# Eleven pairs of experts first, fourteen triples last: a new order of units in a mixture of experts

## What is computed

```python
def _moe(x, p):
    scores = jax.nn.sigmoid(xf @ p['w_router'])
    ...   # group-limited choice of 8 of 64 experts for each token
    def expert_block(args):
        h = silu(einsum('td,edf->tef', xb, w_gate)) * einsum('td,edf->tef', xb, w_up)
        h = h * gb[..., None]
        return einsum('tef,efd->td', h, w_down)
    shared = (silu(xf @ ws_gate) * (xf @ ws_up)) @ ws_down
    return routed + shared
```

## Time and profile before

| | before |
|---|---|
| median of three runs | 1019.37 us |
| lowest and highest | 1017.78, 1020.24 us |
| the profiled execution's own time | 1016.32 us |
| its span, first to last instruction | 1014.5 us |
| TensorE busy (modelled) | 915.6 us, 90% |
| bytes moved | 265.11 MB |
| mean granted TensorE clock | 0.964 |

### The profile page before, as it was taken

One profiled execution on the slowest core, in us unless ns is written; L12 is line 12 of the kernel. 1 busy time (PEld: TensorE's weight loads), 2 busy tenths in 40 slices (PEclk: granted clock), 3 DMA queues, 4 the chain that ended last, 5 costly groups with the idle time before them and its releaser, 6 DMA issues.

```text
span 1014.5 us, 19304 instructions
## 1 busy us (share of the span) xinstructions
PE 915.6 (90%) x7879; PEld 552.0 (54%) x7879; DVE 495.6 (49%) x1030; ACT 230.0 (23%) x478; POOL 243.7 (24%) x280
## 2 busy tenths in 40 slices
PE   4999999999999997779999999978889978798995
PEld 4878877887787777536744434323333333233332
DVE  2148857885787487885624333313322323222325
ACT  3231134113411351244111212111211112111213
POOL 0039904960794099100100000000000000000000
PEclk9999999999999999979999999979989989898999
DMA  8643134214412408139688999999999999999961
GB/s 242 188 125 94 36 122 144 62 44 138 126 55 84 139 2 291 27 145 420 273 340 343 394 419 420 419 420 420 418 419 420 419 420 420 420 419 421 420 281 44
DMA packets 76598, 265.11 MB, mean 261 GB/s; under 512 B 12799, under 2 KB 44097, under 8 KB 51656
## 3 DMA queue, kind: packets, MB, share of 16 engines
q1 hardware_dynamic: 72791, 254.16, 64.7%
q0 software_dynamic: 3712, 9.64, 2.5%
HBM read 263.29 MB, written 5.89 MB: 265 GB/s over the span
## 4 chain that ended last, share of the span: by engine, by line
PE 60%; DMA 19%; SPq 9%; DVE 7%; ACT 2%; issue 2%; DVEq 0%; POOLq 0%; ACTq 0%
PE bank L1368 58%; DMA big<-in_w_up 17%; SPq L403 8%; ACT big L1665 2%; DMA big<-in_w_in 1%; PE bank L637 1%; DVE big L1955 1%; DVE big L2008 1%; DVE big L2012 1%; ACT L1665 1%; DMA big<-xg,big 0%; DVE big L920 0%; DVE big L1203 0%; PE bank L700 0%; SPq L467 0%
## 5 line engine op out<-in xcount | busy, mean ns | idle before, releaser
L1368 PE MATMUL bank<-big 64*64 64x64 f32 (+8 forms) x7422 | 858.5, 377 | 78.2 <-DMA big<-in_w_up 42.5
L1368 PEld LDWEIGHTS bank<-big 64*64 64x64 f32 (+5 forms) x7422 | 498.0, 142 | 421.0 <-issue 348.0
L1665 ACT ACTIVATE big<-bank 128x512 f32<-128x512 f32 (+8 forms) x277 | 118.9, 458 | 622.5 <-PE bank L1368 471.0
L1209 POOL DMA_INDIRECT big<-xg,big x25 | 25.0, 998 | 508.2 <-PE bank L637 402.8
L2154 POOL TENSOR_SCALAR big<-big 128x256 f32<-128x256 f32 x120 | 128.2, 1069 | 0.4
L1072 DVE TENSOR_TENSOR big<-big,bank 128x256 f32<-128x256 f32 x25 | 10.6, 422 | 216.1 <-ACT big L1665 216.1
L2166 POOL TENSOR_TENSOR big<-big 128x256 f32<-128x256 f32 x120 | 87.6, 730 | 0.3
L1955 DVE SCALAR_TENSOR_TENSOR big<-big 128x256 f32<-128x256 f32 x120 | 74.7, 623 | 4.1
L1120 DVE TENSOR_TENSOR big<-big,bank 128x512 f32<-128x512 f32 x100 | 68.7, 688 | 12.6 <-PE bank L1368 11.1
L1013 DVE TENSOR_SCALAR big<-bank 128x1 uint32<-128x1 f32 x25 | 4.0, 159 | 114.1 <-PE bank L1368 114.1
L1665 ACT ACTIVATE big<-big 128x272 f32<-128x272 f32 (+9 forms) x109 | 49.9, 502 | 41.5 <-DVE big L1890 11.3
(11 more groups left out here) (156 smaller groups left out, 360.1 us busy)
## 6 DMA issues: line engine op xcount, KB each, us to landing
big<-in_w_gate SPq DMA_DIRECT2D x64, 1024.0 KB, 22.9
big<-in_w_up SPq DMA_DIRECT2D x64, 1024.0 KB, 27.2
big<-in_w_down SPq DMA_DIRECT2D x64, 1024.0 KB, 27.9
big<-in_w_in SPq DMA_DIRECT2D x29, 1024.0 KB, 5.4
big<-in_w_out SPq DMA_DIRECT2D x2, 2048.0 KB, 12.0
big<-in_state_wkv SPq DMA_DIRECT2D x32, 64.0 KB, 2.2
out_wkv_s<-big SPq DMA_DIRECT2D x32, 64.0 KB, 3.9
big<-in_x_prompt SPq DMA_DIRECT2D x2, 512.0 KB, 3.5
```

What stands on the lines that cost most here:

```text
L1209: pool.indirect_dma_start(out=x[0:n, :], out_offset=None, in_=xg, in_offset=bass.IndirectOffsetOnAxis(ap=idxu[0:n, col:col + 1], axis=0), ...
L1368: return nc.tensor.matmul(out_, lhsT=lhsT, rhs=rhs, start=start, stop=stop)
L1665: return nc.scalar.activation(out_, in_, f, **kw)
```

## The change

`UNITS` becomes eleven pairs and then fourteen triples. `FIRST_T` (11) is the first triple. In triples the order on TensorE is index, **combine(q-1)**, gate_up(q), one piece of the shared down product in each of the first five triples (units 11 to 15), turn_gates(q), turn(q+1), turn_hidden(q), down(q). Pairs keep the order they had. ScalarE turns the next unit's tokens ahead of `hidden_turned` in triples, and VectorE adds the last unit's products ahead of `hidden`. The down weights now go through five slots (n % 5), since the sixth keeps the shared expert's until unit 15; gate and up keep six.

```diff
-UNITS = 'PPP' + 'TTP' * 6 + 'TP' * 2
+UNITS = 'P' * 11 + 'T' * 14
...
-        SHARED_SLOT = 5
+        SHARED_SLOT, NDSLOT = 5, 5
...
         def filled_down(n):
-            return n // NSLOT + 1
+            return n // NDSLOT + 1
...
+        FIRST_T = UNITS.index('T')
...
                 if after:
                     sp.wait_ge(S['h_mm'], u + 1)
-                for n in after:
-                    load_item(sp, 0, n % NSLOT, expert_w(0, which[n + NSLOT]))
-                    load_item(sp, 1, n % NSLOT, expert_w(1, which[n + NSLOT]))
+                for m in after:
+                    load_item(sp, 0, m % NSLOT, expert_w(0, which[m]))
+                    load_item(sp, 1, m % NSLOT, expert_w(1, which[m]))
...
-                if after:
+                if after_down:
                     sp.wait_ge(S['yx_mm'], u + 1)
-                for n in after:
-                    load_item(sp, 2, n % NSLOT, expert_w(2, which.pop(n + NSLOT)))
-                if u == 1:
-                    sp.wait_ge(S['shd_mm'], NDOWN)
-                    load_item(sp, 2, SHARED_SLOT, expert_w(2, SHARED_SLOT))
+                for m in after_down:
+                    load_item(sp, 2, m % NDSLOT, expert_w(2, which.pop(m)))
...
+                if q >= FIRST_T:
+                    combine(q - 1)
+                    gate_up(q)
+                    if q < FIRST_T + NDOWN:
+                        shared_down(q - FIRST_T)
+                    turn_gates(q)
+                    if q + 1 < NU_E:
+                        turn(q + 1)
+                    turn_hidden(q)
+                    down(q)
+                    continue
                 gate_up(q)
...
+                if FIRST_T <= q < LAST:
+                    turned(q + 1)
                 hidden_turned(q)
-                if 1 <= q < LAST:
+                if 1 <= q < FIRST_T:
                     turned(q + 1)
...
+                if q >= FIRST_T:
+                    add_late(q - 1)
                 hidden(q)
...
+                if FIRST_T <= q < FIRST_T + NDOWN:
+                    shared_rows(q - FIRST_T)
                 take_gates(q)
```

More of the change, by code:

```diff
@@ L463, in moe_sp @@
             for u in range(NU_E):
-                after = [n for n in members(u) if n + NSLOT < NE]
-                for n in after:
-                    m = n + NSLOT
-                    which[m] = m if m < NSTATIC else sp.value_load(ids[0:1, m:m + 1], min_val=0, max_val=NE - 1)
+                after = [n + NSLOT for n in members(u) if n + NSLOT < NE]
+                after_down = [n + NDSLOT for n in members(u) if n + NDSLOT < NE]
+                for m in after:
+                    which[m] = sp.value_load(ids[0:1, m:m + 1], min_val=0, max_val=NE - 1)
                 if after:
                     sp.wait_ge(S['h_mm'], u + 1)
-                for n in after:
-                    load_item(sp, 0, n % NSLOT, expert_w(0, which[n + NSLOT]))
-                    load_item(sp, 1, n % NSLOT, expert_w(1, which[n + NSLOT]))
+                for m in after:
+                    load_item(sp, 0, m % NSLOT, expert_w(0, which[m]))
+                    load_item(sp, 1, m % NSLOT, expert_w(1, which[m]))
                 if u == 0:
                     sp.wait_ge(S['shg_mm'], 4)
+                    which[SHARED_SLOT] = SHARED_SLOT
                     for part in range(2):
                         load_item(sp, part, SHARED_SLOT, expert_w(part, SHARED_SLOT))
-                if after:
+                if after_down:
                     sp.wait_ge(S['yx_mm'], u + 1)
-                for n in after:
-                    load_item(sp, 2, n % NSLOT, expert_w(2, which.pop(n + NSLOT)))
-                if u == 1:
-                    sp.wait_ge(S['shd_mm'], NDOWN)
-                    load_item(sp, 2, SHARED_SLOT, expert_w(2, SHARED_SLOT))
+                for m in after_down:
+                    load_item(sp, 2, m % NDSLOT, expert_w(2, which.pop(m)))
             sp.wait_ge(S['cnt_ready'], 1)
@@ L566, in shared_down @@
                 wait(pe, 'shy_ready', n if n < 4 else 0)
-                wait(pe, 'cb_sum', 3 if n == 3 else 0)
+                wait(pe, 'cb_sum', NC * (FIRST_T + n))
                 t, h = divmod(n, 2)
@@ L661, in turn_hidden @@
                     pe.wait_ge(S['shh_ready'], 2)
-                if q == 2:
+                if q == FIRST_T + NDOWN - 1:
                     pe.wait_ge(S['shs_ready'], 6)
@@ L672, in down @@
                 for n in members(q):
-                    pe.wait_ge(S[f'wd_in{n % NSLOT}'], 16 * filled_down(n))
+                    pe.wait_ge(S[f'wd_in{n % NDSLOT}'], 16 * filled_down(n))
                 for h in range(2):
@@ L677, in down @@
                             ins = mm(ps_y[h][lo:lo + w, :], hT[:, j, lo:lo + w],
-                                     slot_w[n % NSLOT][1][:, j, 512 * h:512 * h + 512], j == 0, j == 1)
+                                     slot_w[n % NDSLOT][1][:, j, 512 * h:512 * h + 512], j == 0, j == 1)
                 note(ins, 'yx_mm')
@@ L716, in combine @@
                     else:
-                        if n == 2 and q < 2:
-                            pe.wait_ge(S['shy_ready'], (3, 4)[q])
+                        if n == 2 and 0 <= q - FIRST_T < 4:
+                            pe.wait_ge(S['shy_ready'], q - FIRST_T + 1)
                         ins = mm(comb_bank(q, n), GT[q % NGT][:, 128 * t:128 * t + r],
@@ L732, in moe_pe @@
                     turn(1)
-                    shared_down(0)
                     turn_gates(0)
@@ L736, in moe_pe @@
                     down(0)
-                    shared_down(1)
                     continue
-                if q == 1:
-                    shared_down(2)
                 combine(q - 1)
@@ L743, in moe_pe @@
                 turn_gates(q)
-                if q + 1 < NU_E:
-                    turn(q + 1)
+                turn(q + 1)
                 down(q)
-                if q == 1:
-                    shared_down(3)
-                    shared_down(4)
             with pe.If(count > SLOTS):
@@ L850, in moe_act @@
             for q in range(NU_E):
[L851 to L854, removed]
                 if q == 4:
@@ L862, in moe_act @@
                     turned(1)
+                if q == FIRST_T + NDOWN - 1:
+                    act.wait_ge(S['shd_mm'], NDOWN)
+                    for i in range(4):
+                        note(fn(shs[0:NS, QD * i:QD * i + QD], ps_ss[32 * i:32 * i + NS, :], ACT.Copy), 'shs_ready')
+                if FIRST_T <= q < LAST:
+                    turned(q + 1)
                 hidden_turned(q)
-                if 1 <= q < LAST:
+                if 1 <= q < FIRST_T:
                     turned(q + 1)
@@ L1089, in pair @@
                     v.memset(xq, 0.0)
[L1090 to L1095, removed]
+                if 0 < q < FIRST_T:
+                    add_late(q - 1)
+                if FIRST_T <= q < FIRST_T + NDOWN:
+                    shared_rows(q - FIRST_T)
                 take_gates(q)
```

## The result

The changed kernel takes **1030.95 us** (median of four runs, 1029.14 to 1034.18) against 1019.81 us before (four runs): a ratio of 1.0114 with a 95% interval of 1.009 to 1.0138. Run once more beside the experiments it gave 1.0102 (1.0082 to 1.0122). It is slower, as forecast, and the forecast of 1029 was 2 us low. The profiled execution took 1029.14 us with a span of 1027.3.

What follows compares the result with a forecast made beforehand. TensorE bounds the pairs, idling DMA engines; transfers bound the triples. Data from 705.2 plus 106 matrices (280.4 us) gives 985.6; the work behind makes span 1024.3, 9.8 over the old, so 1019.37 + 9.8 = 1029.2; range 1022 to 1038.

Steps and rivals of the forecast that it cites:

- The two numbers that decide: Whole kernel: how long the DMA engines stand idle, and how much work follows the last weights waited for.
- the prediction's other road: Check assuming never-idle DMA engines from 511.3: 174 matrices at 2.645 us land at 971.5, the kernel ends at 1010.2.
- the prediction's never-idle end: End of kernel had the DMA engines never idled from 511.3 us on: 1010.2 us.
- the prediction's bound: Whole kernel: saved TensorE waits cannot bring the end below 1010.2 us, so are worth 4.3 us at most.
- S(0): Start of down in unit 0: predicted at 516.4 us, 518.33 less the 1.93 us shared block.
- S(10): Start of down in unit 10, the last pair: predicted at 687.7 us, ten pairs of 17.13 us after 516.4.
- the row of 17.13: TensorE's time for a unit in its full part, read from the old profile: 17.13 us, pairs and triples alike.
- Rival 1: Whole stream: transfers run nearer their byte rate, 106 matrices land 5.3 us earlier, giving 1022 to 1026 us; 20%.
- Rival 2: Pairs' stage: DMA engines do not idle there, so the end comes 4.3 us down, at 1015 us; 4%.
- Rival 3: Triples: at a mean clock of 0.75 they become bound by TensorE, giving 1036 to 1046 us; 12%.
- 1.7 us of half clock: Tail: products after the last wait for weights run at half clock, adding 1.7 us.
- the price of the sums ahead at the first triple: Unit 11: combine(10) ahead of gate_up(11) releases SyncE later, so the DMA engines idle 4.6 us more.

Runs made afterwards that it cites:

- The cut in pairs: Changed kernel with the four wide combine products of units 0 to 9 cut from 512 to 64 columns, the rest left out: 1016.92 us.
- the same cut in triples: Changed kernel with the combine products of units 12 to 21 cut from 512 to 64 columns instead: 1030.99 us.
- the sorted kernel with the old ends: Changed kernel with the old order in the first triple, unit 11, and the last two units, 23 and 24: 1024.81 us.
- the two settings: Changed kernel with old order in the first triple: 1026.45 us; old units, late pieces, five slots, new order in triples 3, 4, 6, 7 alone: 1015.12 us.
- the best kernel: Kernel before with only the shared pieces moved to the first five triples and five down slots, old units and order: 1010.10 us.

## Why the prediction was right, point by point

**The two numbers that decide.** Right. The cut in pairs (13.0 us) against the same cut in triples (nothing) shows that idle DMA time in the pairs' stage makes the loss. Ahead of the first data of unit 11 the prediction has 14.0 us of it (705.2 - 511.3, less 68 matrices at 2.645); by the trace it is 15.2 (707.64 - 511.99, less 68 at 2.653). With the cut in pairs the last weights waited for were there 462.1 us behind the first data (975.17 - 511.91 - 1.2), and 174 matrices at 2.653 need 461.6: the engines did not idle, as on the prediction's other road.

Sorting the units costs 14.7 us on otherwise like code, near the 14.1 between the forecast and the prediction's never-idle end, and that is in part luck. In the sorted kernel with the old ends the last wait was over at 988.71, with a first issue at 515.01: 472.5 us behind the first data, so 10.9 us were idling and the rest was not split. And the kernel with the old units and the shared pieces late, whose DMA share is 1.00 from 530 to 580 us, has a span of 1009.0, near the never-idle end of 1010.2, but in another way: its last wait is over at 905.06 with 104 us of TensorE's work behind, not at 971.5 with 38.7. Its way from the first issue to the end is 7.4 us shorter than before (497.2 against 504.6), so the prediction's bound, that the saved waits are worth 4.3 us at most, does not hold for every kernel with these parts.

**The terms** (first of the prediction, then of the profile after):

| term | predicted | measured |
|---|---|---|
| shared piece out of unit 0, from the first transfer to S(0) | 1.9 us less | 8.39 to 6.63, 1.8 less |
| S(0) | 516.4 | 518.6, of it 2.05 ahead of the expert stage |
| one pair | 17.13 | 17.25 |
| DMA share in the pairs' stage | near 0.92 | 0.96 (but 390 of 420 GB/s, which is 0.93) |
| from S(10) to the gate of expert 28 | 16.3 | 16.5 |
| that issue | 704.0 | 707.64 |
| idle gap just ahead of the data | 5 to 6 | 5 (703 to 708) |
| TensorE's time of a triple with a shared piece | 20.5 | 20.58 (732.34 - 711.76) |
| each of 106 matrices, landing | 2.645 | (990.02 - 708.84) / 106 = 2.653 |
| last wait for weights over | 985.6 | 990.0 |
| first triple with a wait on in_w_down | about 15, then 4 to 5 us each | 13 (753.5), then 1.9 to 7.4 us each |
| from the last wait for weights to the end | 38.7 | 37.2 |
| span | 1024.3 | 1027.3 |

The 3.0 us between the spans are 2.05 of chance ahead of the stage, 1.2 in ten pairs, 0.8 in 106 matrices and some tenths, less 1.6 in the tail. A pair followed by a pair takes 0.12 us more than a pair followed by a triple, which is what the row of 17.13 was.

**Rival 1** (transfers at their byte rate) is out: 2.653 us again. **Rival 2** (faster, the pairs never idle) is out: 0.96. **Rival 3** (triples become TensorE's through the clock) is out: TensorE waits for weights in every triple from unit 13 to 23. The cut in triples, at a mean grant of 0.88, moves nothing. The Trainium skill, "TensorE: Matmul & The Clock Gate", section "A second HAM failure mode: psum-queue depth-cycling", says of another kernel that frequent short idles between groups of products made the clock swing. The first two triples have such idles (0.49 and 0.78 us a unit) and no long ones, and the stretch from 691 to 753 us was granted 1.00 throughout, TensorE busy 58.07 of 62 us. In these rows idles of that size left the clock at its upper level; the 0.92 further on goes with waits of 1.9 to 7.4 us.

**The tail** was sized with 1.7 us of half clock. In this execution the products behind the last wait of 1.89 us took 3.64 us, at full clock; in the second profile of the same kernel, behind a wait of 1.57, they took 5.32, and its tail was 38.8 us (1028.7 - 989.90), as predicted. So the term comes in some executions of one kernel and not in others; what decides it no run shows.

**Where I was wrong** is what the parts are worth. The schedule takes all five shared pieces out of the pairs' stage, the first as 1.9 us and the others by counting 17.13 us for units that took 20.9 and 20.2 (539.22 - 518.33 and 559.37 - 539.22), but it never asks what that is worth with the old units. There the late pieces and the five slots give 8.9 us, since they fill the DMA engines' gaps at 544 to 572 us; 5.3 us of it (normalized by the first issue: the share from 975 to 985 us fell from 0.58 to 0.24, which is 3.4, with a start 1.9 later) is in the stream, the rest behind it, which I did not split. And I saw the price of the sums ahead at the first triple (4.6 us predicted, 3.5 and 5.0 measured in the two settings) but priced the tail's share of it in passing.

**The steps of the whole change**: -8.9 for the shared pieces and slots, +14.7 for the sorted units, and +5.1 for the new order at both ends of the triples. These are differences along one row of kernels, so that they add up to the whole (11 us) is no check. On another path the parts are other: the sorted string alone costs 5.9 us, and with sorted units the late pieces and five slots (and the new order in the middle triples) are worth only 0.2 us (1025.01 to 1024.81, on two chips; 1.0 by their ratios, 1.0057 and 1.0047). The late pieces gain with the mixed units, and hardly with the sorted ones.

## What to carry to other kernels

Where two sides (transfers and an engine) take turns at being the bound, a sorted sequence costs the larger side in each stage, and a mixed one at best only the larger of the two sums. Here sorting lost 5.9 us by itself and 14.7 on the best kernel. So keep the mix, and move work, such as the shared pieces here, into stages whose bound is the other side; with the mix that gave 8.9 us. Before a step is put ahead of another on an engine, look at who is released by the one that is put back: in this kernel the new order cost 5 us where the queue was shallow, 3.4 where its engine was the bound, and nothing between. A total of waiting time on the page (42.5 us here) is no store of gains while the transfers are full in the same stretch.

## What the runs showed of the hardware that I had not expected

Landings come slower than bytes. A matrix landed every 2.65 us in both kernels, with 2.50 us of bytes at 420 GB/s and about 0.1 of gathers. At the end of the stream the share of the engines does not drop at once but fades, in the changed kernel around 990.02, where the down matrix of expert 60 has landed and two more are on their way:

```profile
984.00:986.00 2.00, 2.00 (x24) 0.52 (x16) 0.00 (x0) 0.00 (x0) 0.00 (x0) 1.00 1.02 426
986.00:988.00 2.00, 2.00 (x17) 1.44 (x13) 1.14 (x4) 0.90 (x3) 0.00 (x0) 1.00 0.95 397
988.00:990.00 2.00, 0.26 (x2) 0.07 (x1) 1.21 (x5) 0.85 (x3) 0.00 (x0) 1.00 0.74 303
990.00:992.00 2.00, 1.85 (x20) 0.79 (x24) 0.00 (x0) 0.00 (x0) 0.00 (x0) 1.00 0.60 233
992.00:994.00 2.00, 1.79 (x20) 0.34 (x11) 0.00 (x0) 0.15 (x1) 0.00 (x0) 1.00 0.20 82
```

I read this as some engines being done near 986 and others near 993; the view gives the mean of the sixteen only. The Trainium skill, "DMA: Bandwidth & Descriptors", section "Queues, rings and completion order", has each of the 16 engines consume a ring of its own in order; a transfer split over them then counts as landed with the slowest, which fits these rows but is not shown by them. That this spread is the whole of the missing 0.05 us a matrix was not tried.
